# A two-block transformer on one core: the third weight piece after a feed-forward is split behind its residual, and the latent tiles are copied out ahead of the RMS factor

## The chip, the core and the metric

The kernel runs on one core of a Trainium2 chip. The metric is the device time of one execution in microseconds (us). The kernel computes in fp32 accuracy; nothing of it runs on a second core.

## What is computed

The reference is two blocks in a row over 256 tokens of width 1024. Cut to what matters here:

```python
def first_block(x, mem, ...):            # 3 mixers, cross attention, feed-forward 0
    ...
    hf = rms_norm(x, norm_ffn_g[l])
    gate, up = jnp.split(hf @ ffn_w_in[l], 2, axis=-1)     # 1024 -> 2 * 2816
    x = x + (jax.nn.silu(gate) * up) @ ffn_w_out[l]
    return x

def second_block(x, ...):
    for layer in range(2):
        if layer == 0:                   # latent attention and dilated attention
            z = rmsnorm(x, mix_norm_ab[0]) @ w_in_ab[0]    # latent 672, dilated q, k, v 3 * 768
            o_a = mla_mixer(z[..., :IN_A], ...)            # rmsnorm of the q latent (384), kv latent (256)
            o_b = dilated_mixer(z[..., IN_A:], slopes)
            x = x + jnp.concatenate([o_a, o_b], axis=-1) @ w_out_ab[0]
        else:                            # grouped attention
            x = x + gqa_axial_mixer(rmsnorm(x, mix_norm_c[0]), gqa_w_q[0], gqa_w_kv[0], ...)
        x = x + swiglu(rmsnorm(x, ffn_norm[layer]), ffn_w_in[layer], ffn_w_out[layer])
    return rmsnorm(x, final_norm)
```

So there are three feed-forwards, numbered 0, 1 and 2. Feed-forward 0 is followed by the latent and dilated projections, feed-forward 1 by the grouped attention's projections, and feed-forward 2 by the final norm.

## The kernel before

Activations lie transposed, channels on the partitions: `xT` is 8 tiles of 128 channels x 256 tokens and holds the residual stream. Each fp32 product is made of three products of rounded parts (weight high x activation high, weight high x activation low, weight low x activation high), so every weight must be **split** before TensorE can use it. Weights come in pieces of up to 1 MB. SP issues their loads in a fixed order into three `raw` buffers. ScalarE (ACT) rounds half a piece into `whi` (L747, in the loop L1120), and VectorE (DVE) subtracts to get `wlo` (L1312, in the loop L1697). A piece takes two halves on each of the two engines. A `raw` buffer is free for the next load once DVE has made both low halves; `whi` and `wlo` are free once TensorE (PE) has finished the last tile of the piece before in that buffer. The order of the splits is one list made by a small planner, and each engine runs its program in the order in which it is written.

The end of a feed-forward (chunk 10 of 11, `last=True`, then `ffn_tail`): PE finishes the second half of the last chunk's output projection into four PSUM banks, 8 tiles of 128 channels (L1926 to L1928 with `act_hi`, `act_lo`). DVE adds each to `xT` (L1759). ACT scales it by the gain and rounds it into `mem_hi` (L777), DVE makes the low part `mem_lo` (L1622; both are `mem_pair` in the trace), and ACT squares pairs of tiles (L1037), which POOL adds up (L715, L719, L721). PE then starts the next stage's projections, one k (channel tile) after the other as the low parts come. After them comes `norm_sum`, a matmul with ones over POOL's sum, and from it ACT makes the RMS factor `x_rms` of the tokens (L786, L787, L789). The projections run on unnormalised activations; the factor is applied when tiles are copied out, or cancels in a second norm.

Feed-forward tails also hold the splits of the next stage's first three pieces: the first two (`next_split(0)`, `next_split(1)`) inside the last chunk, and the third, half 0 after them and half 1 after the residual. After feed-forward 0 the third piece is ("ab", "lat", 2), 160 columns, so halves of 640 words per partition; after feed-forward 1 it is ("gq", 1), with halves of 1024 words. After feed-forward 2 there is none.

The **latent stage** after feed-forward 0: `project_abreast` makes latent tiles 0 to 3 together, k by k, 96 matmuls, into the four banks of the tile ring. Then come `norm_sum`, tile 4 (which takes the bank of tile 0, so ACT's copy of tile 0 into `lat` must be done), the sums of squares of the q latent, tile 5 (bank of tile 1), and the dilated tiles dq, dk and dv. On ACT, the factor (`x_rms_of(4)`) stands ahead of the loop that copies tiles 0 to 4 (L1179), squares them (L770) and splits the pieces of dq. The **grouped stage** after feed-forward 1: two tiles `gk` abreast (48 matmuls), the first tile of `gq` (24 matmuls), `norm_sum`, and on.

Lines that the steps below use: L747, L1312 (splits), L1759 (residual add after a feed-forward), L777, L1622 (high and low part), L1179 (copies of latent tiles), L786 (factor), L1989 (matmuls with one operand pair, `norm_sum` and the sums of squares among them).

Of the kernel before, what the change touches and what calls it, by code (L numbers as in the profile page):

```python
# [22 lines left out]
ACT = mybir.ActivationFunctionType  # L23
# [3 lines left out]
T = 256  # L27
# [5 lines left out]
CHUNKS = HIDDEN // (2 * P)  # L33
# [245 lines left out]
def build(nc, ins, out, consts, const_at, early_consts):  # L279
# [6 lines left out]
    with ctx:  # L286
# [444 lines left out]
        def _(act):  # L731
# [8 lines left out]
            def split(g, h):  # L740

                landed, free = split_waits(g, h)
                if free is not None:
                    act.wait_ge(tile_done, free)
                act.wait_ge(s_landed[g % SLOTS], landed)
                n = half_words(g)
                act.activation(whi[g % SLOTS][:, h * n:h * n + n], raw[g % SLOTS][:, h * n:h * n + n], ACT.Copy)\  # L747
                   .then_inc(s_split_hi, 1)
# [7 lines left out]
            def tile_in(name, idx):  # L756
                act.wait_ge(tile_done, tile_value(name, idx))
                return ring_bank(name, idx)
# [354 lines left out]
            def feed_forward(f):  # L1113
# [15 lines left out]
                def chunk(i, first=False, last=False):  # L1129
                    t = tile0 + 4 * i - 1 if not first else tile0  # L1130
                    back = 0 if first else 1
                    for j in range(2):
                        e, n = e_hid[:, j, :], 3 * (2 * CHUNKS * f + 2 * i + j)
                        act.wait_ge(s_gate, 2 * CHUNKS * f + 2 * i + j + 1)
                        act.activation(e, gate_hid[:, j, :], ACT.Exp, scale=-1.0).then_inc(s_gate_e, 1)  # L1135
                        act.wait_ge(s_gate_e, n + 1)
                        act.activation(e, e, ACT.Ln, bias=1.0).then_inc(s_gate_e, 1)
                        act.wait_ge(s_gate_e, n + 2)
                        act.activation(e, e, ACT.Exp, scale=-1.0).then_inc(s_gate_e, 1)  # L1139
                        if last and j == 0:  # L1140
                            next_split(0)
                        elif not last:
                            for h in range(2):
                                half(base + 3 + j, h, i, None)
                        if j == (1 if last else 0) and not first:
                            act.wait_ge(tile_done, t + 3 if last else t + 2)
                            half(base + 2, 1, i, None)
                        act.wait_ge(s_ff, 2 * CHUNKS * f + 2 * i + j + 1)
                        act.activation(hid_hi[:, j, :], f_hid[:, j, :], ACT.Copy).then_inc(s_ffhi, 1)
                    if last:  # L1150
                        next_split(1)
                    act.wait_ge(tile_done, t + back + 3)
                    if last:
                        if base + 3 * CHUNKS + 2 < len(pieces):
                            split(base + 3 * CHUNKS + 2, 0)
                    else:
                        half(base + 5, 0, i, None)

                chunk(0, first=True)
# [4 lines left out]
            def ffn_tail(f, n):  # L1164

                residual_in(n)
                g = plan.ffn_piece[f] + 3 * CHUNKS + 2
                if g < len(pieces):
                    split(g, 1)

            feed_forward(0)
            ffn_tail(0, 4)
            x_rms_of(4)


            for i in range(6):
                if i < 5:
                    b = tile_in("lat", i)
                    act.activation(lat[:, i, :], b[:, 0:T], ACT.Copy).then_inc(ev["act"], 1)  # L1179
                after("lat", i)  # L1180
                if i in (1, 2, 4):
                    act.wait_ge(ev["act"], plan.evac["lat", i][1])
                if i == 1:
                    squares(("lat", 0), 0, lat_flat(0, 2), 512)
                if i == 2:
                    squares(("lat", 0), 1, lat_flat(2, 3), T)
                if i == 4:
                    squares(("lat", 1), 0, lat_flat(3, 5), 512)
                    rms_from(("lat", 0))
            rms_from(("lat", 1))  # L1190
            for j in range(3):
                a, b = LAT_TILES[j]
# [102 lines left out]
        def _(dve):  # L1295
# [394 lines left out]
            def feed_forward(f, n):  # L1690
# [17 lines left out]
                def chunk(i, first=False, last=False):  # L1708
# [34 lines left out]
                           .then_inc(s_fflo, 1)  # L1743
                    if last:
                        next_split(1)
                        if base + 3 * CHUNKS + 2 < len(pieces):
                            split(base + 3 * CHUNKS + 2, 0)
                    else:
                        k_ += 1
                        half(base + 5, 0, done + k_)  # L1750
# [13 lines left out]
                    x_low(n, KC - 1)  # L1764
                g = base + 3 * CHUNKS + 2
                if g < len(pieces):
                    split(g, 1)

            feed_forward(0, 4)
# [153 lines left out]
        def _(pe):  # L1923
# [486 lines left out]
            project_abreast(4, [("lat", i, ("ab", "lat", i // 2), P * (i % 2)) for i in range(4)])  # L2410
            norm_sum(4)
            project("lat", 4, ("ab", "lat", 2), 0, XN)
            sum_squares(("lat", 0), 0, bank[4][:, 0:T], 2, True, False)
            sum_squares(("lat", 0), 1, bank[4][:, 0:T], 1, False, True)
            project("lat", 5, ("ab", "lat", 2), 64, XN, cols=96)
            for n in ("dq", "dk"):
                for i in range(6):
                    project(n, i, ("ab", n, i // 2), P * (i % 2), XN)
# [238 lines left out]
```

## Time and profile before

| what | value |
|---|---|
| median of 3 runs | 1244.26 us (1241.68 to 1246.94) |
| profiled execution: span | 1242.8 us (the page gives no other time of it) |
| PE busy | 1143.5 us, 92% |
| DVE busy | 843.2 us, 68% |
| ACT busy | 622.1 us, 50% |
| chain of work that ended last | PE 75%, DVE 12%, ACT 8% |
| core's mean granted TensorE clock | 0.962 of full |
| feed-forward 0 ends on PE, next stage starts | 531.1, 534.86 us |
| feed-forward 1 ends on PE, next stage starts | 915.7, 922.91 us |

All times inside the run are counted from the span's start. The span runs from the first to the last instruction of the one profiled execution; the median of the runs shown is 1.5 us above it. A granted clock of 1.00 is 2.4 GHz, and of 0.50 is 1.2 GHz. Idle time of an engine that isn't the bottleneck costs nothing, so what counts is where PE stands still or is slowed, and on whom it waits there.

### The profile page before, as it was taken

The page shows a single profiled execution, that of the slowest core. Times are in us where ns is not written, and L with a number is a line of the kernel's source. Part 1 is how long each engine was busy: PE and PEld are TensorE (multiplying, and loading weights), DVE is VectorE, ACT ScalarE, POOL GpSimd, SP SyncE. Part 2 cuts the span into 40 slices and gives each one's busy share as a digit, 9 for nine tenths or more (in the row PEclk, how much of TensorE's full clock was granted, in tenths as well). Part 3 has the DMA queues.
Part 4 walks back from the last instruction along what each step waited for, and adds up shares of the span by engine and source line. Part 5 has one row for each costly group of instructions (what it writes and reads, how often), then busy time and mean ns, then how long its engine had stood idle before and what let it go on. Part 6 is the DMA issues. An engine that isn't in the chain of part 4 may idle for free.

```text
span 1242.8 us, 20747 instructions
## 1 busy us (share of the span) xinstructions
PE 1143.5 (92%) x7968; PEld 1016.9 (82%) x7968; DVE 843.2 (68%) x1271; ACT 622.1 (50%) x1106; POOL 39.5 (3%) x40
## 2 busy tenths in 40 slices
PE   4899899898999999989988899999978889999998
PEld 4787678698889999989965679999976668999997
DVE  3776675356578778856456477787875657877875
ACT  4634245555455545554454354454554475554544
POOL 2000000010010000010000010000010001000000
PEclk8998799999999999989999899999989899999998
DMA  8333221335266666456430055666675404576650
GB/s 251 123 116 103 68 69 68 102 97 175 69 187 195 203 184 184 139 158 188 130 94 1 3 167 175 166 201 202 178 127 136 102 1 142 163 203 190 181 170 34
DMA packets 218144, 169.18 MB, mean 136 GB/s; under 512 B 20787, under 2 KB 208098, under 8 KB 217954
## 3 DMA queue, kind: packets, MB, share of 16 engines
q1 hardware_dynamic: 216962, 164.44, 45.5%
q0 software_dynamic: 496, 2.43, 0.6%
q10 hardware_dynamic: 624, 1.44, 0.4%
q8 instruction: 45, 0.74, 0.3%
q14 instruction: 17, 0.14, 0.0%
HBM read 167.24 MB, written 1.05 MB: 135 GB/s over the span
## 4 chain that ended last, share of the span: by engine, by line
PE 75%; DVE 12%; ACT 8%; issue 2%; DMA 1%; SPq 1%; POOL 0%; POOLq 0%; ACTq 0%; DVEq 0%
PE bank L2350 19%; PE bank L1989 12%; PE bank L1926 10%; PE bank L1927 10%; PE bank L1928 10%; PE bank L2352 9%; DVE wlo L1312 4%; DVE arena L1305 2%; ACT whi L747 2%; PE bank L1983 1%; PE bank L1985 1%; PE bank L1984 1%; ACT arena L1260 1%; SPq L678 1%; DVE hf L1323 1%
## 5 line engine op out<-in xcount | busy, mean ns | idle before, releaser
L2350 PE MATMUL bank<-mem_pair,whi 128*128 128x512 f32 x1056 | 377.3, 400 | 2.5 <-DVE mem_pair L1622 1.6
L2352 PE MATMUL bank<-mem_pair,wlo 128*128 128x256 f32 x1056 | 296.9, 281 | 0.0
L1926 PE MATMUL bank<-act_hi,whi 128*128 128x256 f32 (+1 forms) x920 | 266.4, 290 | 15.9 <-DVE act_lo L1331 4.7
L1927 PE MATMUL bank<-act_lo,whi 128*128 128x256 f32 (+1 forms) x920 | 262.8, 286 | 0.0
L1928 PE MATMUL bank<-act_hi,wlo 128*128 128x256 f32 (+1 forms) x920 | 262.6, 285 | 0.0
L1312 DVE TENSOR_TENSOR wlo<-raw,whi 128x1024 fp32r<-128x1024 f32 (+3 forms) x137 | 162.5, 1227 | 133.5 <-ACT whi L747 132.4
L2350 PEld LDWEIGHTS bank<-mem_pair,whi 128*128 128x128 f32 x1056 | 198.9, 188 | 49.6 <-DVE mem_pair L1622 2.7
L1697 DVE TENSOR_TENSOR wlo<-raw,whi 128x1024 fp32r<-128x1024 f32 x177 | 208.9, 1221 | 4.0
L2352 PEld LDWEIGHTS bank<-mem_pair,wlo 128*128 128x128 f32 x1056 | 200.1, 189 | 0.1
L1926 PEld LDWEIGHTS bank<-act_hi,whi 128*128 128x128 f32 (+1 forms) x920 | 177.3, 193 | 27.8 <-issue 12.0
L1120 ACT ACTIVATE whi<-raw 128x1024 fp32r<-128x1024 f32 x180 | 179.8, 1045 | 0.4 <-PE bank L1928 0.4
L1927 PEld LDWEIGHTS bank<-act_lo,whi 128*128 128x128 f32 (+1 forms) x920 | 177.4, 193 | 0.8 <-issue 0.7
L1928 PEld LDWEIGHTS bank<-act_hi,wlo 128*128 128x128 f32 (+1 forms) x920 | 177.5, 193 | 0.0
L1989 PE MATMUL bank<-arena 32*32 32x256 f32 (+9 forms) x1052 | 138.3, 392 | 24.1 <-DVE arena L1323 6.7
L1135 ACT ACTIVATE arena<-arena 128x256 f32<-128x256 f32 x66 | 27.6, 418 | 253.8 <-DVE arena L1305 253.8
L747 ACT ACTIVATE whi<-raw 128x1024 fp32r<-128x1024 f32 (+3 forms) x134 | 129.8, 1018 | 26.9 <-PE bank L1928 17.7
L1721 DVE TENSOR_REDUCE arena<-bank 128x256 f32<-128x512 f32 x132 | 90.7, 687 | 76.2 <-PE bank L2352 76.2
L1989 PEld LDWEIGHTS bank<-arena 32*32 32x32 f32 (+5 forms) x1052 | 83.6, 137 | 64.4 <-issue 17.2
L1305 DVE TENSOR_TENSOR arena<-arena 128x256 f32<-128x256 f32 (+5 forms) x190 | 95.3, 503 | 40.5 <-ACT arena L1139 21.3
L1926 PE MATMUL bank<-mem_pair,whi 128*128 128x256 f32 (+1 forms) x352 | 109.8, 312 | 13.1 <-DVE mem_pair L1622 11.0
L1927 PE MATMUL bank<-mem_pair,whi 128*128 128x256 f32 (+1 forms) x352 | 104.3, 296 | 0.0
L1928 PE MATMUL bank<-mem_pair,wlo 128*128 128x256 f32 (+1 forms) x352 | 103.9, 295 | 0.0
(215 smaller groups left out, 1318.8 us busy)
## 6 DMA issues: line engine op xcount, KB each, us to landing
raw<-in_ffn_w_in_dram SPq DMA_DIRECT2D x132, 512.0 KB, 5.2
raw<-in_ffn_w_out_dram SPq DMA_DIRECT2D x33, 1024.0 KB, 5.0
raw<-in_w_in_ab_dram SPq DMA_DIRECT2D x11, 1024.0 KB, 5.7
raw<-in_w_in_dram SPq DMA_DIRECT2D x9, 1024.0 KB, 7.1
raw<-in_xa_wk_dram SPq DMA_DIRECT2D x4, 1024.0 KB, 5.5
raw<-in_xa_wv_dram SPq DMA_DIRECT2D x4, 1024.0 KB, 5.1
raw<-in_w_out_dram SPq DMA_DIRECT2D x4, 1024.0 KB, 5.1
raw<-in_xa_wq_dram SPq DMA_DIRECT2D x4, 1024.0 KB, 5.0
```

What stands on the lines that cost most here:

```text
L747: act.activation(whi[g % SLOTS][:, h * n:h * n + n], raw[g % SLOTS][:, h * n:h * n + n], ACT.Copy)\
L1120: act.activation(whi[slot][:, h * 1024:h * 1024 + 1024], raw[slot][:, h * 1024:h * 1024 + 1024], ACT.Copy).then_inc(s_split_hi, 1)
L1305: return dve.tensor_tensor(dst, a, b, ALU.mult)
L1312: dve.tensor_tensor(wlo[g % SLOTS][:, at_], raw[g % SLOTS][:, at_], whi[g % SLOTS][:, at_].bitcast(F32), ALU.subtract).then_inc(s_split_lo, 1)
L1697: dve.tensor_tensor(wlo[slot][:, at_], raw[slot][:, at_], whi[slot][:, at_].bitcast(F32), ALU.subtract)\
L1721: dve.tensor_reduce(x[:, j, :], bank[2 * j + g][:].rearrange("p (h t) -> p t h", h=2), AX.X, ALU.add)\
L1926: pe.matmul(dst, w[0], a[0], start=start, stop=False, **kw)
L1927: pe.matmul(dst, w[0], a[1], start=False, stop=False, **kw)
L1928: return pe.matmul(dst, w[1], a[0], start=False, stop=stop, **kw)
L1989: return pe.matmul(dst, w, a, start=start, stop=stop, skip_group_check=True)
L2350: pe.matmul(b[:].rearrange("p (h t) -> p h t", h=2), w[0][:, k, g, :], mem_pair[:, :, k, :], start=k == 0, stop=False, skip_group_check=True)
L2352: last = pe.matmul(b[:, 0:T], w[1][:, k, g, :], mem_hi[:, k, :], start=False, stop=k == KC - 1, skip_group_check=True)
```

## The change

1. The third piece's half 0 is no longer split inside the last chunk, on ACT and on DVE; it is split after the residual, right ahead of half 1. ACT's wait for `tile_done` ahead of it goes too in the last chunk.
2. ACT copies the latent tiles 0 to 3 before it makes the factor. The squares of the q latent come next, then the splits that stood between the copies, then the copy of tile 4 and its squares, then the splits after tile 5, and only then the root of the q latent's mean square (`rms_from(("lat", 0))`).
3. PE makes latent tile 5 before the q latent's sums of squares, not after them.

```diff
@@ ACT, feed_forward, chunk @@
                     if last:
                         next_split(1)
-                    act.wait_ge(tile_done, t + back + 3)
-                    if last:
-                        if base + 3 * CHUNKS + 2 < len(pieces):
-                            split(base + 3 * CHUNKS + 2, 0)
                     else:
+                        act.wait_ge(tile_done, t + back + 3)
                         half(base + 5, 0, i, None)
@@ ACT, ffn_tail @@
                 residual_in(n)
                 g = plan.ffn_piece[f] + 3 * CHUNKS + 2
                 if g < len(pieces):
+                    split(g, 0)
                     split(g, 1)
 
             feed_forward(0)
             ffn_tail(0, 4)
+            def lat_out(i):
+                b = tile_in("lat", i)
+                act.activation(lat[:, i, :], b[:, 0:T], ACT.Copy).then_inc(ev["act"], 1)
+
+            for i in range(4):
+                lat_out(i)
             x_rms_of(4)
-            for i in range(6):
-                if i < 5:
-                    b = tile_in("lat", i)
-                    act.activation(lat[:, i, :], b[:, 0:T], ACT.Copy).then_inc(ev["act"], 1)
-                after("lat", i)
-                if i in (1, 2, 4):
-                    act.wait_ge(ev["act"], plan.evac["lat", i][1])
-                if i == 1:
-                    squares(("lat", 0), 0, lat_flat(0, 2), 512)
-                if i == 2:
-                    squares(("lat", 0), 1, lat_flat(2, 3), T)
-                if i == 4:
-                    squares(("lat", 1), 0, lat_flat(3, 5), 512)
-                    rms_from(("lat", 0))
+            act.wait_ge(ev["act"], plan.evac["lat", 2][1])
+            squares(("lat", 0), 0, lat_flat(0, 2), 512)
+            squares(("lat", 0), 1, lat_flat(2, 3), T)
+            after("lat", 1)
+            after("lat", 3)
+            lat_out(4)
+            act.wait_ge(ev["act"], plan.evac["lat", 4][1])
+            squares(("lat", 1), 0, lat_flat(3, 5), 512)
+            after("lat", 5)
+            rms_from(("lat", 0))
             rms_from(("lat", 1))
@@ DVE, feed_forward, chunk @@
                     if last:
                         next_split(1)
-                        if base + 3 * CHUNKS + 2 < len(pieces):
-                            split(base + 3 * CHUNKS + 2, 0)
@@ DVE, feed_forward, after the residual @@
                 g = base + 3 * CHUNKS + 2
                 if g < len(pieces):
+                    split(g, 0)
                     split(g, 1)
@@ PE, latent stage @@
             norm_sum(4)
             project("lat", 4, ("ab", "lat", 2), 0, XN)
+            project("lat", 5, ("ab", "lat", 2), 64, XN, cols=96)
             sum_squares(("lat", 0), 0, bank[4][:, 0:T], 2, True, False)
             sum_squares(("lat", 0), 1, bank[4][:, 0:T], 1, False, True)
-            project("lat", 5, ("ab", "lat", 2), 64, XN, cols=96)
```

In the order of instructions of the changed kernel, lines after the first edit are 1 to 4 lower in number (L1757 is L1759 of before, L1175 is L1179). On DVE, at the end of feed-forward 0, where the residual begins, the rows were before:

```order
L1312 TENSOR_TENSOR wlo<-raw,whi 128x1024 x2
L1312 TENSOR_TENSOR wlo<-raw,whi 128x640
L1759 TENSOR_TENSOR xT<-xT,bank 128x256 x2
L1622 SCALAR_TENSOR_TENSOR mem_pair<-xT,col,mem_pair 128x256
L1759 TENSOR_TENSOR xT<-xT,bank 128x256
```

and with the change:

```order
L1312 TENSOR_TENSOR wlo<-raw,whi 128x1024 x2
L1757 TENSOR_TENSOR xT<-xT,bank 128x256 x2
L1622 SCALAR_TENSOR_TENSOR mem_pair<-xT,col,mem_pair 128x256
L1757 TENSOR_TENSOR xT<-xT,bank 128x256
L1622 SCALAR_TENSOR_TENSOR mem_pair<-xT,col,mem_pair 128x256
```

The 640-word half that stood between the second piece's halves and the first residual add now stands behind the last low part, as one of two. After feed-forward 1 the same holds with a half of 1024 words.

On ACT, from the last high part of the residual on, before:

```order
L1037 ACTIVATE hf<-xT 128x512
L747 ACTIVATE whi<-raw 128x640
L786 ACTIVATE x_eps<-bank 128x256
L787 ACTIVATE rms<-bank,eps 128x256
L789 ACTIVATE x_rms<-rms 128x256
L1179 ACTIVATE arena<-bank 128x256 x2
L747 ACTIVATE whi<-raw 128x1024 x2
L770 ACTIVATE sq<-arena 128x512
L1179 ACTIVATE arena<-bank 128x256
L770 ACTIVATE sq<-arena 128x256
L1179 ACTIVATE arena<-bank 128x256
L747 ACTIVATE whi<-raw 128x1024 x2
```

and with the change:

```order
L1037 ACTIVATE hf<-xT 128x512
L747 ACTIVATE whi<-raw 128x640 x2
L1175 ACTIVATE arena<-bank 128x256 x4
L786 ACTIVATE x_eps<-bank 128x256
L787 ACTIVATE rms<-bank,eps 128x256
L789 ACTIVATE x_rms<-rms 128x256
L770 ACTIVATE sq<-arena 128x512
L770 ACTIVATE sq<-arena 128x256
L747 ACTIVATE whi<-raw 128x1024 x4
L1175 ACTIVATE arena<-bank 128x256
L770 ACTIVATE sq<-arena 128x512
L747 ACTIVATE whi<-raw 128x1024 x2
```

`arena<-bank` are the copies of the latent tiles. Four of them now stand ahead of the factor (`x_eps`, `rms`, `x_rms`), and four halves of split stand together behind the squares. SP's and POOL's orders are the same.

## Rows read from the trace of the kernel before

**Rows 1.** The page's head: span and instructions.
```profile
span 1242.8 us, 20747 instructions
```
**Rows 2.** Chain of waits, end of feed-forward 0: start, us, what.
```profile
527.53 4.09 DMA raw<-in_w_in_ab_dram
531.73 0.74 ACT whi L747
532.50 0.82 DVE wlo L1312
```
**Rows 3.** Chain of waits, end of feed-forward 1.
```profile
914.01 4.94 DMA raw<-in_gqa_w_q_dram
919.06 1.06 ACT whi L747
920.14 1.23 DVE wlo L1312
```
**Rows 4.** Timeline of DVE, end of feed-forward 0: start, us, line, count [idle before].
```profile
527.76 2.35 DVE L1312 TENSOR_TENSOR wlo<-raw,whi 128x1024 fp32r<-128x1024 f32 x2
533.24 0.75 DVE L1759 TENSOR_TENSOR xT<-xT,bank 128x256 f32<-128x256 f32 x2
```
**Rows 5.** Timeline of DVE, end of feed-forward 1.
```profile
912.34 2.35 DVE L1312 TENSOR_TENSOR wlo<-raw,whi 128x1024 fp32r<-128x1024 f32 x2
...
921.29 0.75 DVE L1759 TENSOR_TENSOR xT<-xT,bank 128x256 f32<-128x256 f32 x2
...
927.51 1.57 DVE L1622 SCALAR_TENSOR_TENSOR mem_pair<-xT,col,mem_pair 128x256 fp32r<-128x256 f32 x2
930.04 1.47 DVE L1312 TENSOR_TENSOR wlo<-raw,whi 128x1024 fp32r<-128x1024 f32 x1 [0.96 <-ACT whi L747]
```
**Rows 6.** Timeline of PE, from the end of feed-forward 0 to the dilated tiles.
```profile
528.18 0.28 PE L1927 MATMUL bank<-act_lo,whi 128*128 128x256 f32 x1
...
530.82 0.28 PE L1928 MATMUL bank<-act_hi,wlo 128*128 128x256 f32 x1
534.86 0.55 PE L1926 MATMUL bank<-mem_pair,whi 128*128 128x256 f32 x1 [3.77 <-DVE mem_pair L1622]
535.21 0.41 PE L1927 MATMUL bank<-mem_pair,whi 128*128 128x256 f32 x1
...
539.05 0.41 PE L1927 MATMUL bank<-mem_pair,whi 128*128 128x256 f32 x1
...
548.67 0.59 PE L1989 MATMUL bank<-x_sum,ones 128*128 128x256 f32 x2
550.91 0.36 PE L1926 MATMUL bank<-mem_pair,whi 128*128 128x256 f32 x1 [1.65 <-ACT arena L1179]
...
565.16 0.39 PE L1926 MATMUL bank<-mem_pair,whi 128*128 128x256 f32 x1
```
**Rows 7.** Timeline of PE, start of the grouped stage.
```profile
922.91 0.55 PE L1926 MATMUL bank<-mem_pair,whi 128*128 128x256 f32 x1 [7.23 <-DVE mem_pair L1622]
...
934.31 0.59 PE L1989 MATMUL bank<-x_sum,ones 128*128 128x256 f32 x2
```
**Rows 8.** Busy time by stretch: length, PE, PEld, DVE, ACT, POOL, PEclk, DMA share, GB/s.
```profile
534.90:548.00 13.10, 13.10 (x91) 13.10 (x92) 7.48 (x14) 5.53 (x11) 5.17 (x4) 0.81 0.44 134
...
922.80:925.00 2.20, 2.09 (x10) 2.12 (x11) 2.20 (x7) 1.98 (x5) 0.04 (x1) 0.50 1.35 217
...
927.00:929.00 2.00, 2.00 (x11) 2.00 (x11) 2.00 (x4) 1.49 (x4) 1.39 (x1) 0.50 0.34 55
...
935.00:937.00 2.00, 0.27 (x1) 0.27 (x2) 0.00 (x0) 1.97 (x6) 0.00 (x0) 1.00 0.46 161
```
**Rows 9.** Timeline of ACT, the factor and the first latent copies.
```profile
549.30 0.38 ACT L786 ACTIVATE x_eps<-bank 128x256 f32<-128x256 f32 x1 [7.65 <-PE bank L1989]
...
550.40 0.64 ACT L1179 ACTIVATE arena<-bank 128x256 f32<-128x256 f32 x2
```
**Rows 10.** Timeline of POOL, the last add after feed-forward 0 and after 1.
```profile
542.46 1.20 POOL L721 TENSOR_TENSOR x_sum<-x_sum 128x256 f32<-128x256 f32 x1
...
930.50 1.60 POOL L721 TENSOR_TENSOR x_sum<-x_sum 128x256 f32<-128x256 f32 x1
```

## The prediction

> **What bounds the kernel now.** I read the chain of waits first, since it says which engine a microsecond must be taken from; then the timelines of DVE, PE and ACT at the two places where the change moves something; then the busy time by stretch, for the clock. The span is 1242.8 us [rows 1].
>
> The chain is PE's nearly everywhere, but it leaves PE at both feed-forward tails. After feed-forward 0 it goes to the load of the third piece, ACT's split of its half 0, DVE's split, and only then to the residual [rows 2]. On DVE, the two halves of the second piece end at 527.76 + 2.35 = 530.11 and the first residual add begins at 533.24 [rows 4]. What stands between is a half that waited for its load; PE needs it only for latent tile 4. Meanwhile PE stands still for 3.77 us [rows 6]. After feed-forward 1 the same place is worse: the load ends at 914.01 + 4.94 = 918.95, ACT and DVE take 1.06 and 1.23 [rows 3], DVE had been free since 912.34 + 2.35 = 914.69, the residual begins at 921.29 [rows 5], and PE stands still for 7.23 us [rows 7].
>
> Each pause also costs clock. At full clock a matmul follows the one before it after 0.12 us: 22 steps from 528.18 to 530.82. Behind the pause it is 0.213 us: 18 steps from 535.21 to 539.05 [rows 6]. The stretch of the four latent tiles ran at a mean clock of 0.81; after feed-forward 1 the clock stood at 0.50 (1.2 GHz) at 922.8 and still up to 929 [rows 8].
>
> The third place is in the latent stage. PE makes norm_sum at 548.67, and tile 4 starts at 550.91 after 1.65 us of idleness, released by ACT's copy of a tile [rows 6]. Tiles 0 to 3 were done by 548.67, but ACT made the factor first, from 549.30 to 550.40 [rows 9].
>
> **The change, part by part.**
>
> *Half 0 of the third piece moves behind the residual, after feed-forward 0.* The first add needs output tiles 0 and 1, six matmuls of 24: those of the last half begin just before 528.18, so they are there by 529. DVE therefore begins at 530.11, not 533.24: 3.13 us earlier. The eight tiles take DVE 7.8 us (921.29 to 929.08 after feed-forward 1, rows 5), 0.97 each, and PE ends the eighth at 531.1, so no add waits for PE. ACT's part comes between them as before. PE's first latent matmul moves from 534.86 to 531.73, a pause of 0.64 us. Would the clock fall in it? No row has this very gap, so I bound it: a fall costs as much as now, no fall costs nothing. The nearest row, and even a harder case, is the stretch 935 to 937, where PE was idle for 1.73 of 2.00 us and the clock stayed at 1.00 [rows 8]. I take no fall. The 96 matmuls then need 96 x 0.12 = 11.52 us and end at 543.25, where before they ended at 548.67. That is 5.42 us: 3.13 from the start, 2.29 from the clock. DVE and ACT keep up: four tiles abreast take 1.44 us per k, their pace is 0.97.
>
> *The half itself.* It costs ACT 0.74 and DVE 0.82 us [rows 2], now at 538 to 541 instead of on the path. Tile 4 needs it at 543.8. Cost nothing; if the cover went, 0.8. The load's landing (531.6) covers nothing any more, with 6 us to spare. SP's queue: the raw buffer of this piece is free only when its second half is split, and that comes earlier, not later.
>
> *The copies ahead of the factor.* Tiles 0 to 3 end 0.36 us apart. A copy takes 0.32 (two in 0.64, rows 9), so tile 0 is out before PE has made norm_sum, and PE goes straight on: minus 1.65 us. The factor comes after all four copies, about 0.1 us later relative to norm_sum; its first user is far behind.
>
> *The order behind it.* PE takes tile 5 before the sums of squares: same work, no wait either way. PE reaches dq at about 550.8. Its piece: the factor ends at 543.9 + 1.1 = 545.0, then two squares, two halves on ACT (2.1) and one more on DVE (1.2), so 548.3 plus the squares, each at most half as wide as a half of a piece (0.5). Ready at 549.3, 1.5 us ahead. The q latent's root now stands behind two more halves on ACT; PE's sums of squares of the kv latent wait for it, at about 553.7, and by the same sum it comes at 553.5. So near that I hold between 0 and 1 us for it; I take 0. PE's matmul at 565.16 [rows 6] should come near 558.1: this stage gives 5.42 + 1.65 = **7.1 us**. Behind it PE runs without a break, and its splits wait for PE's buffers, not for loads, so nothing takes the gain back.
>
> *After feed-forward 1.* The residual begins at 914.69 instead of 921.29, 6.6 us earlier. PE begins at 922.91 - 6.6 = 916.3, 0.64 us after its last matmul. Two tiles abreast need only 0.72 us per k, less than DVE's 0.97, so here DVE sets the end: the last low part ends at 927.51 + 1.57 = 929.08, shifted to 922.5. The last k adds 0.72, the first gq tile 24 x 0.12 = 2.88: norm_sum at 926.1, not 934.31 [rows 7]. That is **8.2 us**, of which 1.6 come from the clock.
>
> *What is late next there.* POOL's last add ended at 930.50 + 1.60 = 932.10 [rows 10]; shifted, 925.5, with 0.6 us in hand. DVE now has two halves beside it instead of one. The row of the one that stood there before: 1.47 us beside POOL's add against 1.23 alone [rows 5, 3], and POOL's 1.60 beside it against 1.20 after feed-forward 0 [rows 10]. Each is held up by some 0.2 to 0.4, so I take nothing. The Trainium skill, "SBUF — State Buffer", section "SBUF: two separate sides", says that VectorE (with two SBUF inputs) and GpSimd lock a shared port pair for a whole instruction, and the other fully blocks. By that rule a second half of 1.23 us could push POOL's end to 926.7 and norm_sum by 0.6, and the sum would be 14.7 instead of 15.3; the rows above don't decide it, as overlap hides part of a block.
>
> The pieces of gq loaded next: loads run until 929 at the latest (DMA share 0.34 in 927 to 929, rows 8), and the split of the last of them moves to 934. They are in time. Feed-forward 2 has no third piece, so nothing changes there.
>
> **Sum.** 7.1 + 8.2 = 15.3 us off a span of 1242.8, so 1227.5. The median of the runs is 1.5 us above that span, so I predict 1244.3 - 15.3 = **1229.0 us**.
>
> **The rivals.**
>
> *The clock falls anyway.* For it: in the grouped stage PE is fed at DVE's pace and so stands still for about a quarter of the time, in small gaps, and at both places the clock fell behind a gap. Against it: the row of 935 to 937. Then the latent stage gives 3.13 + 1.65 = 4.8, and the grouped one 6.6 if it is low for as long as now: 11.4, so 1232.9. If all 72 matmuls ran at 0.213, norm_sum would come at 931.7 and the grouped stage give 2.6: 7.4, so 1236.9. The Trainium skill, "TensorE: Matmul & The Clock Gate", section "A second HAM failure mode: psum-queue depth-cycling", tells of a kernel whose clock swung because TensorE idled briefly but often between groups; by that rule this rival would hold in the grouped stage. 0.19.
>
> *A new wait in the latent stage or at POOL.* Root behind the splits (up to 1 us) and POOL's lock (0.6), or a piece of dq late by another 1: gives back up to 2.6, so 1229.6 to 1231.6. For it: margins of 0.2 and 0.6 us. 0.10.
>
> *The gain is taken back by loads.* If the stages behind were fed by loads at their limit, an earlier start would wait for them, as the third piece did. Then only a part stays, 0 to 6 us: 1238 to 1244. Against it: loads begin when buffers come free, which moves with the rest. 0.05. That the change doesn't do what it says (the residual still behind a load) is excluded by the order of instructions on DVE; PE's claim of the third piece stands 12 us behind its landing.
>
> *Slower: the rests kept the clock up.* PE has 10.9 us less rest. If the clock were granted for rest, PE would be throttled in the feed-forwards, where it is the bound. At 0.213 instead of 0.12 each low microsecond costs 0.44, so the point from which it decides is 35 us of low clock: above that the gain is gone, and 60 us would give 1229 + 26 = 1255. Against it: low stretches in this trace follow idleness, and full ones follow work. 0.02.
>
> **How the numbers follow.** My case 0.64, clock 0.19, new wait 0.10, loads 0.05, slower 0.02. A gain of 0.5% (6.2 us), about what a measurement of this kernel can tell from no change, is passed by the first three; of the loads' case nearly all lies within it. Faster 0.93, same 0.05, slower 0.02. The range: below 1229 the runs' own scatter (1241.68 against a median of 1244.26) and a low stretch less later on, about 5 us; above, the clock's and the wait's cases, and the scatter: 1224 to 1235.
>
> **What would show it.** Right: after feed-forward 0 PE's pause before the latent tiles is 0.6 us and the clock 1.00 through it; DVE's residual directly follows its second piece; the wait on ACT's copy ahead of tile 4 is gone; after feed-forward 1 PE's pause falls from 7.23 to about 0.6 and norm_sum comes 11.4 - 1.6 = 9.8 us after PE's start. Wrong: a clock of 0.50 in either stage, PE waiting at L1989 for ACT's root or for POOL, or a stage behind that takes longer than before.

## The result and the profile after

The changed kernel took 1224.18 us in the median of 4 runs (1223.54 to 1225.34). In the same comparison the kernel before took 1242.97 (4 runs, 1236.2 to 1246.94). The ratio on record is 0.9881 with a 95% interval of 0.9836 to 0.9925. It is not the quotient of these two medians, which is 0.985 (18.8 us). In a second comparison, with more runs, the changed kernel took 1223.51 us (6 runs, 1222.62 to 1224.31) against 1238.76 (29 runs, 1233.15 to 1248.73), a ratio of 0.9869 (0.9824 to 0.9914). The gain is 15.3 us between those medians, and between 10.7 and 21.8 us by the interval. The profiled execution took 1223.7 us, with this span:

```profile
span 1221.7 us, 20745 instructions
```

Against [rows 1] that is 21.1 us less, more than the runs gained. Where the rest comes from is shown below.

On VectorE, at the end of feed-forward 0 and then of feed-forward 1 (start, us, line, count, idle before), the rows that answer to [rows 4, 5]:

```profile
524.47 2.35 DVE L1312 TENSOR_TENSOR wlo<-raw,whi 128x1024 fp32r<-128x1024 f32 x2
526.74 0.74 DVE L1757 TENSOR_TENSOR xT<-xT,bank 128x256 f32<-128x256 f32 x2
...
898.92 2.35 DVE L1312 TENSOR_TENSOR wlo<-raw,whi 128x1024 fp32r<-128x1024 f32 x2
901.19 0.74 DVE L1757 TENSOR_TENSOR xT<-xT,bank 128x256 f32<-128x256 f32 x2
...
907.42 1.58 DVE L1622 SCALAR_TENSOR_TENSOR mem_pair<-xT,col,mem_pair 128x256 fp32r<-128x256 f32 x2
909.97 3.16 DVE L1312 TENSOR_TENSOR wlo<-raw,whi 128x1024 fp32r<-128x1024 f32 x2 [0.97 <-ACT whi L747]
```

The residual adds now follow the second piece with no time between: 524.47 + 2.35 = 526.82, and the first add starts at 526.74. The third piece's two halves stand behind the last low part.

In the chain of waits no load is left at either tail (after feed-forward 0 it goes from the second piece's split, 524.56 + 2.27 us, straight to the residual). After feed-forward 1 it now reads as follows, against [rows 3]:

```profile
897.44 1.23 DVE wlo L1312
898.67 0.34 DVE act_lo L1742
899.00 2.27 DVE wlo L1312 x2
901.27 0.34 DVE xT L1757
```

What sets the residual's start there is the second piece's split on VectorE.

On PE, the answers to [rows 6, 7]:

```profile
528.36 0.36 PE L1925 MATMUL bank<-mem_pair,whi 128*128 128x256 f32 x1 [0.56 <-DVE mem_pair L1622]
...
539.95 0.59 PE L1988 MATMUL bank<-x_sum,ones 128*128 128x256 f32 x2
...
554.06 0.60 PE L1988 MATMUL bank<-ones,x_rms 1*128 1x2 f32 x4
...
902.81 0.36 PE L1925 MATMUL bank<-mem_pair,whi 128*128 128x256 f32 x1 [0.55 <-DVE mem_pair L1622]
906.49 0.39 PE L1925 MATMUL bank<-mem_pair,whi 128*128 128x256 f32 x1 [0.58 <-DVE mem_pair L1622]
908.66 0.39 PE L1925 MATMUL bank<-mem_pair,whi 128*128 128x256 f32 x1 [0.46 <-DVE mem_pair L1622]
913.07 0.59 PE L1988 MATMUL bank<-x_sum,ones 128*128 128x256 f32 x2
```

The pause of 3.77 us is 0.56, and the one of 7.23 is 0.55. From norm_sum to the next norm factor's columns PE has no wait left. In the grouped stage two small waits on VectorE's low parts appear. The answers to [rows 8] (length, PE, PEld, DVE, ACT, POOL, PEclk, DMA share, GB/s):

```profile
528.00:540.00 12.00, 11.64 (x97) 11.67 (x98) 9.20 (x16) 7.49 (x16) 5.21 (x4) 1.00 0.60 183
...
904.00:908.00 4.00, 3.42 (x28) 3.20 (x27) 3.95 (x9) 3.29 (x7) 2.40 (x2) 1.00 1.35 218
908.00:913.00 5.00, 4.54 (x38) 4.34 (x37) 4.03 (x4) 2.57 (x4) 3.23 (x3) 1.00 1.35 219
```

The clock is 1.00 through both stages. The waits in the grouped stage come from low parts that took longer while a POOL add ran. For the last wait the add ran from 906.90 to 908.33 us, and the low part compares with the next one so:

```profile
907.42 1.19 DVE L1622 SCALAR_TENSOR_TENSOR mem_pair<-xT,col,mem_pair 128x256 fp32r<-128x256 f32 x1
...
908.53 0.47 DVE L1622 SCALAR_TENSOR_TENSOR mem_pair<-xT,col,mem_pair 128x256 fp32r<-128x256 f32 x1
```

On ScalarE and POOL, the answers to [rows 9, 10]:

```profile
539.07 1.46 ACT L1175 ACTIVATE arena<-bank 128x256 f32<-128x256 f32 x4 [3.27 <-PE bank L1927]
540.58 0.38 ACT L786 ACTIVATE x_eps<-bank 128x256 f32<-128x256 f32 x1
```
```profile
910.44 1.61 POOL L721 TENSOR_TENSOR x_sum<-x_sum 128x256 f32<-128x256 f32 x1
```

To see where the 21.1 us of the two profiles come from, and for every run below, I cut each trace at the same PE rows. The stretches are: **A** start to the norm_sum of the first cross attention; **B** on to feed-forward 0's norm_sum; **C** to PE's first latent matmul; **D** to the latent stage's norm_sum; **E** to the columns of the factor (L1989 with `x_rms`); **F** to PE's start in feed-forward 1; **G** to its start in the grouped stage; **H** to norm_sum there; **I** to the columns there; **J** to feed-forward 2's norm_sum; **K** to the end. All are differences of starts in us. "before" and "changed" are the two profiles told of so far, "again" is a second profile of the changed kernel, and the others are the experiments.

```
            A      B      C      D      E      F      G      H      I      J      K
before    275.4   70.5  188.9   13.8   16.0  160.8  197.5   11.4   14.9   96.8  196.8
changed   272.2   70.5  185.7   11.6   14.1  158.1  190.7   10.3   14.9   97.2  196.6
again     272.6   70.5  185.7   11.6   14.1  158.1  190.7   10.3   14.9   97.1  196.6
e_move    276.8   70.5  185.7   11.6   16.0  163.4  190.6   10.3   14.9   97.1  196.5
e_lat     270.1   70.5  189.1   14.0   14.1  163.4  197.2   11.3   13.4   97.4  196.6
e_fill    270.1   70.5  189.1   11.6   16.0  163.8  197.2   10.3   14.9   97.2  196.6
e_move0   268.9   70.5  185.8   11.6   16.0  164.1  197.2   11.3   13.4   97.4  196.6
e_move1   267.3   72.1  189.0   13.1   16.0  160.8  190.9   10.3   14.9   97.2  196.6
e_peorder 272.5   70.5  185.7   11.6   14.1  160.8  190.2   10.3   13.4   96.8  196.7
v_fill    268.8   70.5  185.7   11.6   14.1  162.4  190.5   10.3   13.4   96.2  197.3
d_after4  275.4   70.5  185.7   11.6   15.0  164.3  190.6   10.3   14.9   97.1  196.5
d_after8  268.9   72.1  185.7   11.6   15.9  162.7  190.6   10.3   14.9   97.1  196.5
d_after12 273.6   70.5  185.7   11.6   16.8  162.5  190.5   10.3   14.9   97.1  196.5
d_before8 273.7   70.5  189.0   13.7   17.8  162.8  197.4   11.3   13.4   97.4  196.5
```

Between the first two rows, the stretches that the change touches give C 3.2, D 2.2, E 1.9, G 6.8 and H 1.1, 15.2 us together. A and F give 3.2 and 2.7 more, 5.9 us, and nothing in them was changed.

The same profiles show when the clock falls at the two places. Over the pauses of 0.55 to 0.62 us ahead of the latent or the grouped stage, 18 in ten profiles, there is no low clock in the stage behind (D or H). Over the eight unfilled pauses of 3.8 to 7.4 us there is some in every one: 3.4 to 6.1 us of the stage at 0.50.

### The profile page after: what moved, and what is told of

It is laid out like the page before. It is cut to its first block, busy times and chain, and to the rows that moved or that the text cites. A ratio compares the mean times of both kernels' runs of the same rounds, so it can differ in the third digit from the quotient of the medians.

```text
span 1221.7 us, 20745 instructions
## 1 busy us (share of the span) xinstructions
PE 1133.3 (93%) x7968; PEld 1009.3 (83%) x7968; DVE 843.6 (69%) x1271; ACT 621.9 (51%) x1106; POOL 39.6 (3%) x40
## 4 chain that ended last, share of the span: by engine, by line
PE 75%; DVE 13%; ACT 8%; issue 2%; SPq 1%; DMA 1%; POOLq 0%; POOL 0%; DVEq 0%; ACTq 0%
PE bank L2349 19%; PE bank L1988 12%; PE bank L1925 10%; PE bank L2351 10%; PE bank L1926 10%; PE bank L1927 10%; DVE wlo L1312 4%; DVE arena L1305 2%; ACT whi L747 2%; PE bank L1982 1%; PE bank L1983 1%; PE bank L1984 1%; ACT arena L1260 1%; SPq L678 1%; DVE hf L1323 1%
## 5 line engine op out<-in xcount | busy, mean ns | idle before, releaser
L1312 DVE TENSOR_TENSOR wlo<-raw,whi 128x1024 fp32r<-128x1024 f32 (+3 forms) x137 | 163.3, 1235 | 114.4 <-ACT whi L747 113.3
L1988 PE MATMUL bank<-arena 32*32 32x256 f32 (+9 forms) x1052 | 134.0, 387 | 24.1 <-DVE arena L1323 6.7
L1925 PE MATMUL bank<-mem_pair,whi 128*128 128x256 f32 (+1 forms) x352 | 107.2, 305 | 2.6 <-DVE mem_pair L1622 2.2
L1926 PE MATMUL bank<-mem_pair,whi 128*128 128x256 f32 (+1 forms) x352 | 101.6, 289 | 0.0
L1927 PE MATMUL bank<-mem_pair,wlo 128*128 128x256 f32 (+1 forms) x352 | 101.4, 288 | 0.0
```

The source lines that it names most:

```text
L1312: dve.tensor_tensor(wlo[g % SLOTS][:, at_], raw[g % SLOTS][:, at_], whi[g % SLOTS][:, at_].bitcast(F32), ALU.subtract).then_inc(s_split_lo, 1)
L1925: pe.matmul(dst, w[0], a[0], start=start, stop=False, **kw)
L1926: pe.matmul(dst, w[0], a[1], start=False, stop=False, **kw)
L1927: return pe.matmul(dst, w[1], a[0], start=False, stop=stop, **kw)
L1988: return pe.matmul(dst, w, a, start=start, stop=stop, skip_group_check=True)
```

## The experiments

### The changed kernel again

> The changed kernel itself, again, to narrow the interval and to see how far its times scatter. Theory (the prediction's sum of 15.3 us plus what the clock adds by chance elsewhere): 14 to 19 us faster than before. Its own scatter should be small (before: 1236.2 to 1246.94; changed kernel so far 1223.54 to 1225.34) if what scatters in the kernel before is the clock behind the two pauses; it should be as wide as that of before, some 10 us, if the scatter comes from elsewhere.

Measured: 1223.51 us against 1238.76, as above, 15.3 us less. Its six runs lie within 1.7 us, those of before within 15.6. So the first guess of that text, that the scatter comes from the clock behind the two pauses, looked right at this point. The runs at the end of this section don't bear it out.

### The change's two halves apart

**e_move** has the third piece's half moved and nothing else. **e_lat** has the latent stage's new order and nothing else.

```diff
 # e_move, against before: ACT and DVE, last chunk
-                        if base + 3 * CHUNKS + 2 < len(pieces):
-                            split(base + 3 * CHUNKS + 2, 0)
 # and behind the residual
                 if g < len(pieces):
+                    split(g, 0)
                     split(g, 1)
```
```diff
 # e_lat, against the changed kernel: the split of half 0 back in the last chunk
-                    split(g, 0)
                     split(g, 1)
```

> Only the third piece's half 0 moved behind the residual, at both feed-forwards; copies, factor and PE's order as before. Theory: all but the 1.65 us of the copy, so 13.6 us faster by the prediction's sum; PE's idle time ahead of latent tile 4 stays at 1.65 us. Rival (the copies and PE's order carry more than the one wait): clearly less than 12.

Measured: 1228.70 us in the median of 12 runs (1226.0 to 1235.38), ratio 0.9922 (0.9892 to 0.9952). That is 10.1 us less, not 13.6. PE's wait ahead of tile 4 is still there:

```profile
546.80 0.36 PE L1923 MATMUL bank<-mem_pair,whi 128*128 128x256 f32 x1 [1.65 <-ACT arena L1177]
```

In the table above, C, D, G and H are those of the changed kernel and E is that of before, to 0.1 us. So the profile has the whole step of 3.2 + 2.2 + 6.9 + 1.1 = 13.4 us, while the medians show 10.1. The ratio's interval, 5.9 to 13.4 us, ends at the step: the runs just allow its size and don't confirm it. The rival's number (clearly less than 12) came in the medians, but its cause did not: E, where the copies and PE's order act, holds 1.9 us and no more.

> Only the latent stage's new order (copies ahead of the factor, tile 5 ahead of the sums of squares); the third piece split where it was. Theory: 1.65 us faster, which the runs can hardly tell from nothing; in the profile the wait on the copy ahead of tile 4 is gone and the pauses of 3.8 and 7.2 us stay. Rival: with the third piece's second half coming late (543.1), tile 4 now waits for it instead and nothing is gained.

Measured: 1238.96 us (12 runs, 1235.89 to 1243.81), ratio 1.0004 (0.9973 to 1.0035). No change, as far as the runs tell. In the profile tile 4 follows norm_sum at once, while the pauses of 3.9 and 7.2 us stay:

```profile
543.66 0.59 PE L1991 MATMUL bank<-x_sum,ones 128*128 128x256 f32 x2
543.90 0.47 PE L1928 MATMUL bank<-mem_pair,whi 128*128 128x256 f32 x1
```

Stretch E falls from 16.0 to 14.1. The rival, that tile 4 would now wait for the split, falls: there is no such wait. But 1.9 us can't be seen in the sum of a run: the interval goes from 3.3 us faster to 4.3 us slower.

### The clock's share alone

**e_fill** leaves the kernel before as it is and keeps PE busy in both pauses.

```diff
+            keep_clock(14, 0)
             project_abreast(4, [("lat", i, ("ab", "lat", i // 2), P * (i % 2)) for i in range(4)])
...
+            keep_clock(30, 0)
             project_abreast(6, [("gk", k, ("gkv", 0), P * k) for k in range(2)])
```

> The kernel before, with 14 and 30 matmuls of ones into a free bank ahead of the latent and of the grouped stage, so that PE is busy in both pauses while the residuals stay as late as before. Theory: the clock stays at 1.00 through both stages, and norm_sum comes 2.3 us earlier in the latent stage and 1.6 us in the grouped one: 3.9 us faster. Rival (the clock fell for another reason, or its fall cost nothing there): clock of 0.50 in the stages as before and no gain.

Measured: 1240.97 us (12 runs, 1234.27 to 1244.06), ratio 1.0006 (0.9976 to 1.0035): no gain. Yet in its profile the mechanism is there. The first and third row lie in the filled pauses, the others in the stages behind them:

```profile
525.80:529.60 3.80, 2.99 (x27) 2.82 (x27) 2.11 (x5) 1.91 (x4) 0.00 (x0) 1.00 1.11 369
529.60:541.00 11.40, 11.40 (x95) 11.40 (x96) 7.54 (x14) 5.57 (x11) 5.20 (x4) 1.00 0.36 104
911.00:918.20 7.20, 6.74 (x61) 6.57 (x60) 2.51 (x5) 2.22 (x4) 0.00 (x0) 1.00 1.23 213
918.20:928.40 10.20, 9.16 (x72) 8.76 (x73) 7.61 (x14) 5.90 (x11) 5.61 (x4) 1.00 0.54 114
```

The residuals are as late as before (C 189.1, G 197.2), the clock is 1.00, and D falls from 13.8 to 11.6 and H from 11.4 to 10.3: the values of the changed kernel. So the 2.2 and 1.1 us are the price of the clock, apart from the start. The runs don't show them: the interval ends at 3.0 us faster, just short of 3.3. In this profile F takes 163.8 us, against 160.8 of before. Whether F took the gain back in the other runs too is not shown.

### Each tail alone

**e_move0** moves the half after feed-forward 0 only, **e_move1** after feed-forward 1 only.

```diff
 # e_move0 (e_move1: f == 1), ACT and DVE, last chunk and tail
-                        if base + 3 * CHUNKS + 2 < len(pieces):
+                        if f != 0 and base + 3 * CHUNKS + 2 < len(pieces):
                             split(base + 3 * CHUNKS + 2, 0)
...
+                    if f == 0:
+                        split(g, 0)
                     split(g, 1)
```

> Half 0 of the third piece moved behind the residual after feed-forward 0 only. Theory: 5.4 us faster (3.1 of start, 2.3 of clock); PE's pause there 0.6 us, and after feed-forward 1 still 7.2. Rival (the clock falls in a later gap instead and takes the 2.3 back): 3.1.

Measured: 1233.38 us (10 runs, 1232.62 to 1239.5) against 1237.02 (23 runs), ratio 0.9965 (0.9935 to 0.9994), so 3.6 us between the medians and 0.7 to 8.0 us by the interval. In the profile C and D give 3.1 + 2.2 = 5.3, and G and H stay. The rival, a later fall of the clock that takes the 2.2 back, did not come in D.

> The same after feed-forward 1 only. Theory: 8.2 us faster (6.6 of start, 1.6 of clock). Rival: 6.6, or less if POOL's sum is held up by VectorE's two halves.

Measured: 1234.36 us (10 runs, 1226.51 to 1242.42), ratio 0.9957 (0.9913 to 1.0), so 2.7 us in the medians and 0 to 10.8 us by the interval. In the profile G and H give 6.6 + 1.1 = 7.7. Here the runs scatter over 16 us, so this median says little of a step of 8.

### PE's order alone

**e_peorder** is the changed kernel with PE's old order of tile 5 and the sums of squares.

```diff
             project("lat", 4, ("ab", "lat", 2), 0, XN)
-            project("lat", 5, ("ab", "lat", 2), 64, XN, cols=96)
             sum_squares(("lat", 0), 0, bank[4][:, 0:T], 2, True, False)
             sum_squares(("lat", 0), 1, bank[4][:, 0:T], 1, False, True)
+            project("lat", 5, ("ab", "lat", 2), 64, XN, cols=96)
```

> The changed kernel with PE's old order: the sums of squares of the q latent ahead of tile 5. Theory: the squares are out before PE ends tile 4, so it doesn't wait and the time is that of the changed kernel within the scatter. Rival (PE's order is needed): PE idle at the sums by the time that two halves of split on ScalarE take, 2 us.

Measured: 1225.58 us (4 runs, 1223.88 to 1227.99). E is 14.1 as in the changed kernel, and the sums follow tile 4's last matmul with no wait:

```profile
543.45 0.28 PE L1927 MATMUL bank<-mem_pair,wlo 128*128 128x256 f32 x1
...
543.56 1.24 PE L1988 MATMUL bank<-sq,ones 128*128 128x256 f32 x5
```

So PE's order is worth nothing by itself in this stretch; the copies ahead of the factor carry the 1.9 us.

### Filling the grouped stage's waits

**v_fill** is the changed kernel with matmuls of ones in PE's two waits behind the grouped norm_sum.

```diff
                         if i == 0:
                             norm_sum(6)
+                            keep_clock(8, 6)
...
+                if i == 0:
+                    keep_clock(9, 6)
                 g_swapped(i)
```

> The changed kernel with 8 matmuls of ones behind the grouped stage's norm_sum and 9 ahead of its first rotation, into a free bank, to fill PE's waits of 1.8 and 2.2 us there. Theory: the low clock that followed them (3.4 us at 0.50) goes, 1.5 us faster than the changed kernel. Rival: the fill delays the work behind it, or the low stretch moves elsewhere: same or slower.

Measured: 1223.22 us (6 runs, 1220.04 to 1226.78), that is 0.3 us under the 1223.51 of the changed kernel, within the scatter of both. In the profile the low stretch behind these waits is gone and I falls from 14.9 to 13.4. But e_peorder's I is 13.4 too, with no fill. It is no version that can be told from the changed kernel.

### What the scatter is

By now the same step showed fully in every profile and unevenly in the runs. The table points to A and F above all: no experiment touches the code in them, and A ranges from 267.3 to 276.8 us, F from 158.1 to 164.3. (I, at 13.4 or 14.9, and B, at 70.5 or 72.1, move a little too.) Summed from the clock of each of the 14 profiles, A has 23.9 us at half clock where it is shortest and 44.4 where it is longest, and F 6.8 and 23.9. That is some 0.4 us of time for each us at half clock, and it accounts for A and F to about 1 us in all 14.

All edits stand behind A, so they can hardly be what moved it. It goes with the moment of the clock's first fall. That came at 21.1 us in before and d_after4, and A is 275.4 in both. It came at 22.2 and 22.3 us in e_move0 and d_after8, and A is 268.9 in both. In e_fill and e_lat it came at 23.0 and 23.1 us, and A is 270.1 in both. Small shifts count for much: in the changed kernel's first profile it came at 21.2 us, and A is 272.2.

Within F, two profiles show what differs. In the dilated attention, the same 12 matmuls, behind the same waits of 0.69 us, took 5.38 us in the kernel before and 2.80 in the changed one (the clock fell in the rows left out, at 696.9 us):

```profile
695.29 1.09 PE L2509 MATMUL bank<-cst,arena 128*128 128x128 f32 x8 [2.31 <-DVE arena L1305]
...
698.20 5.38 PE L1989 MATMUL bank<-arena 128*64 128x256 f32 x12 [0.69 <-ACT arena L1229]
```
```profile
684.79 1.09 PE L2508 MATMUL bank<-cst,arena 128*128 128x128 f32 x8 [2.31 <-DVE arena L1305]
...
687.48 2.80 PE L1988 MATMUL bank<-arena 128*64 128x256 f32 x12 [0.69 <-ACT arena L1229]
```

The clock of the first was 0.50, of the second 1.00:

```profile
696.90:703.70 6.80, 5.99 (x16) 2.80 (x14) 0.00 (x0) 0.85 (x3) 0.00 (x0) 0.50 0.00 0
```
```profile
686.10:690.30 4.20, 3.46 (x16) 1.98 (x16) 0.00 (x0) 1.07 (x2) 0.00 (x0) 1.00 0.00 0
```

What the engine had done before was the same in both: the same 12 matmuls one round earlier, at 690.17 and 679.68 us, took 2.80 in both, again behind 0.69. So the clock's rise and fall don't depend on the work alone. If they depend on when the work comes, a shift of everything by a microsecond or two should change the time by more than itself. **d_after4**, **d_after8** and **d_after12** test this on the changed kernel, **d_before8** on the one before, with nothing but a delay in a stretch where PE never waits:

```diff
             project("lat", 5, ("ab", "lat", 2), 64, XN, cols=96)
+            keep_clock(8, 6)
```

> The changed kernel with 4 matmuls of ones behind latent tile 5, in a stretch where PE never waits: everything behind comes 0.85 us later. Theory (unchanged stretches lose more or less to low clock according to where they fall against the clock's own rhythm): the time follows the low clock, 0.44 us for each low microsecond, not the delay; medians of this and the two longer delays lie between 1223 and 1232 and not in the order of their delays, and the scatter may be far wider than the changed kernel's 2 us. Rival (additive): 1224.4 with its narrow scatter.

> The same with 8 matmuls, 1.7 us of delay. Theory as for 4. Rival (additive): 1225.2 with a narrow scatter.

> The same with 12 matmuls, 2.6 us of delay. Theory as for 4. Rival (additive): 1226.1 with a narrow scatter.

> The kernel before with 8 matmuls of ones behind latent tile 5, 1.7 us of delay and nothing else. Theory: its scatter, 1233 to 1249, changes with the delay, and its median may even fall below that of the kernel before. Rival (additive): median 1.7 us up, the same two groups of times.

Measured, with the delay that stretch E shows:

```
            delay   median us   lowest    highest   runs
again        0      1223.51     1222.62   1224.31    6
d_after4     0.9    1228.09     1220.24   1233.97    5
d_after8     1.8    1228.99     1227.84   1235.38   11
d_after12    2.7    1230.14     1226.46   1235.46   10
before       0      1235.76     1233.43   1246.40   26  (same comparison as the delays)
before       0      1238.76     1233.15   1248.73   29  (same comparison as "again")
d_before8    1.8    1244.28     1239.23   1248.83   11
```

The additive rival falls for the kernel before. Of its 26 runs in the same comparison, 15 took 1233.4 to 1236.3 us. With the delay of 1.8 us none of 11 runs came under 1239.2. So the delay did not move two groups of times by 1.8 us; the lower group is gone. The median rose by 8.5 us, but the size is loose: the ratio is 1.0046 (1.0014 to 1.0079), 1.7 to 9.8 us, and would by itself just admit 1.8.

For the changed kernel the case is weaker, since it was not run without a delay in that comparison. Its 1.7 us of scatter come from another chip and six runs, and the delays' runs scatter over 7.5 to 13.7 us. The chip by itself is not the likely reason: the kernel before has its lowest run at 1233.2, 1233.7 and 1233.4 us in three comparisons on three chips. The medians came in the order of the delays, which I had not expected, and the steps behind the first, 0.9 and 1.15 us, are near the delays' own. What a delay can't have changed is A, which lies ahead of it. In the three profiles F is 4.4 to 6.2 us longer than in the changed kernel.

Within one kernel the time follows the low clock: of the 29 runs of before, those with a mean clock of 0.972 took 1233.15 to 1235.91 us, those with 0.962 took 1244.05 to 1245.36. Of a span of some 1240 us that is 2 x 0.010 x 1240 = 25 us more at half clock for some 10 us of time, 0.4 us for each.

The change's worth can be taken a second time from these runs. With the same delay of 1.8 us on both sides, d_before8 less d_after8 is 1244.28 - 1228.99 = 15.3 us, and without a delay it is 1238.76 - 1223.51 = 15.3. That the two agree to 0.1 us is chance: each of these medians can be off by several us.

## Why the prediction was right

The forecast was 1229.0 us in a range of 1224 to 1235, and faster. The measured 1224.18 lies 0.2 us inside the range's lower edge, 4.8 us under the forecast, and the second comparison's 1223.51 lies outside. That the range held is luck; the steps are what was right. One by one:

- **The residual's start.** Forecast 3.13 and 6.6 us; measured 3.2 in C and 6.8 in G. The pause was put at 0.64 us and is 0.56 and 0.55. Right.
- **The clock in the latent stage.** Forecast 2.29 us and no fall; measured 2.2 and a clock of 1.00, and e_fill shows it apart from the start. Before, 5.0 us of D ran at 0.50, so each cost 0.44 us, the prediction's price.
- **The clock in the grouped stage.** Forecast 1.6 us; measured 1.1. The step "the last k adds 0.72" failed by half a microsecond. The low part of the k before the last came late too: it took 1.19 us beside POOL's add and ended at 908.61, and PE waited 0.46 us for it. PE then needed 0.72 us for that k and 0.72 for the last, whose low part ended at 909.00. Before, 6.1 us of H ran at 0.50 and cost only 1.1, since VectorE sets the pace there. The mechanism held, the size was off.
- **The copy ahead of tile 4.** Forecast 1.65; E fell by 1.9. From norm_sum's start to that of tile 4 it was 550.91 - 548.67 = 2.24 us and is 540.19 - 539.95 = 0.24. The 1.65 us leave out the time for which norm_sum counts as busy, and a tile needn't wait for that. The latent stage's whole gain was put at 7.1 us and is 7.3 (C, D and E), the grouped one's at 8.2 and is 7.9 (G and H). PE's new order was put at no gain, and e_peorder shows none. No wait on the root came.
- **POOL and the port.** POOL's last add took 1.61 us against 1.60, ended at 912.05, and norm_sum at 913.07 didn't wait for it. VectorE paid: its two halves took 3.16 us, where two alone take 2.35. After feed-forward 0 the two smaller halves took 2.68 beside POOL's adds, where two take 2 x 0.82 = 1.64 by the prediction's row. By the Trainium skill's rule of the locked port pair ("SBUF — State Buffer", section "SBUF: two separate sides") one of the two must wait for the other, and the 0.8 and 1.0 us agree with that. The push on POOL that the prediction estimated by that rule, 0.6 us, did not come; the sum of 15.3 stood.
- **The rivals.** The clock did not fall behind the shorter pauses, nor in the grouped stage with its small waits (rows of 904 to 913, clock 1.00), so the Trainium skill's swinging clock ("TensorE: Matmul & The Clock Gate", section "A second HAM failure mode: psum-queue depth-cycling") is not seen there. Loads took nothing back: J and K stayed within 0.4 us of before, and G kept the whole shift. The throttled feed-forward did not come. (That rival's 10.9 us of rest is a slip: 3.13 + 6.59 + 1.65 is 11.4. Nothing hangs on it.)

So the sum of 15.3 us was met: 15.2 in the stretches of the profiles, 15.3 in the second comparison's medians, whose interval is wide (10.7 to 21.8). What was off by 4.8 us is the number it was taken from. The step "the median of the runs is 1244.3" rested on 3 runs; 29 runs have a median of 1238.76, and 1238.76 - 15.3 is 1223.5, near the measured time. The same comparison's own four runs of before have 1242.97, from which it would be 1227.7. "The runs' own scatter" was put at about 5 us; it is 15.6 us for the kernel before, and the profiled execution, with a mean clock of 0.962, was one of its slower ones.

What stays open: the parts measured one by one come short in the medians (10.1 for 13.4 in e_move, 0 for 3.3 in e_fill, 2.7 for 7.7 in e_move1). The intervals of e_move0, e_move1 and e_lat hold their steps, e_move's ends at its step, and e_fill's ends just short of it. In the profiles the low clock in A and F makes up for such differences, but the other runs have only a mean clock, so where each of them lost it is not known. Nor is it known why the changed kernel's ten runs stayed within 3 us, and what makes the clock fall at another moment in one execution than in the next.

## What to carry to other kernels

An instruction that waits for a load holds up everything behind it in its engine's order, so a split for later use should stand behind the work on the path even if its input is expected in time; look for the engine that stood free while the chain went through a DMA. A pause of several us costs its own length and then low clock behind it: 0.44 us for each us at half clock where TensorE sets the pace, and less where another engine does (1.1 for 6.1 here). A run with the pause filled shows that part by itself. Where unchanged stretches differ by several microseconds between profiles, add up only those that the change touches, and judge a small step by its stretch, not by a median: a step of 2 us showed as nothing in one median here (e_lat), and as 8.5 us in another (d_before8).

## What the runs showed of the hardware that was not expected

The clock's falls don't follow from the work alone: the same 12 matmuls with the same waits took 5.38 or 2.80 us. The start of the program alone, up to the first norm_sum of cross attention, took 267.3 to 276.8 us over 14 profiles, with 23.9 to 44.4 us of it at half clock, though no edit reaches it. Moving all later work of the kernel before by 1.8 us raised its median by 8.5 us (1.7 to 9.8 by the ratio's interval). Of 18 pauses of 0.55 to 0.62 us ahead of the two stages none brought a low clock in the stage behind, and all eight of 3.8 us and more did. VectorE's splits beside POOL's adds took 3.16 us for two where two alone take 2.35, and a low part beside an add took 1.19 against 0.47. POOL's last add took 1.61 us beside two halves and 1.60 beside one.
